# Gate groups moved between the up-projection tiles, one-hot rows built on VectorE, low parts on GpSimd

## What is computed

```python
s = jnp.einsum('thpd,hpnd->thpn', q, sub_keys).astype(jnp.float32)
sv, si = lax.top_k(s, K)
cand = (sv[:, :, 0, :, None] + sv[:, :, 1, None, :]).reshape(T, H, K * K)
...
best, pos = lax.top_k(cand, K)
...
gate = jax.nn.softmax(best, axis=-1).astype(x.dtype)
...
    a = jnp.einsum('chkd,cd->chk', expert_u[ec], xc)
    w = gc * jax.nn.gelu(a, approximate=False)
    return jnp.einsum('chk,chkd->cd', w, expert_v[ec])
```

## Time and profile before

| | |
|---|---|
| median of 3 runs | 2197.05 us (2192.01 to 2198.41) |
| span of the profiled execution | 2194.3 us (its device time is not listed apart; the median lies 2.75 us above the span) |
| PE busy | 2136.5 us, 97% of the span |
| DVE, ACT, POOL busy | 68%, 53%, 8% of the span |
| up-projection of layer 1 | 296 to 664 us of the span |
| gate stage of layer 1 | 664 to 746 us |
| down-projection of layer 1 | 746 to 1088 us |

### The profile page before, as it was taken

How to read it: one execution, slowest core, us unless ns; L and a number is a source line. 1 busy time by engine, 2 the same in 40 slices (tenths; PEclk the granted TensorE clock), 3 DMA queues, 4 the chain that set the end, 5 groups by cost and what they waited for, 6 DMA issues and landing times.

```text
span 2194.3 us, 41496 instructions
## 1 busy us (share of the span) xinstructions
PE 2136.5 (97%) x14244; PEld 1917.2 (87%) x14244; DVE 1500.2 (68%) x2796; ACT 1156.8 (53%) x1835; POOL 181.5 (8%) x202
## 2 busy tenths in 40 slices
PE   8999999999999999999999999999999999999997
PEld 6987899999997788888788888999999977888886
DVE  6666767777778855555676566777777797555556
ACT  4456445544458755445444464444544596444443
POOL 1100000000007400000020000000000182000000
PEclk9999999999999999999999999999999999999999
DMA  5622455555550256666565234555555503665664
GB/s 187 198 86 88 155 165 182 182 183 183 182 180 27 59 191 193 201 203 198 160 197 167 88 106 154 166 183 183 183 183 182 166 0 101 195 201 191 200 204 134
DMA packets 97584, 350.24 MB, mean 160 GB/s; under 512 B 11312, under 2 KB 11344, under 8 KB 97520
## 3 DMA queue, kind: packets, MB, share of 16 engines
q1 hardware_dynamic: 94320, 338.69, 48.3%
q0 software_dynamic: 3200, 10.66, 1.6%
HBM read 348.26 MB, written 1.05 MB: 159 GB/s over the span
## 4 chain that ended last, share of the span: by engine, by line
PE 85%; DMA 4%; DVE 4%; ACT 2%; issue 2%; POOL 1%; POOLq 0%; DVEq 0%; SPq 0%; ACTq 0%
PE wide L1536 33%; PE acc L1521 13%; PE acc L1522 13%; PE acc L1523 13%; PE acc L2003 4%; DMA raw<-in_front 2%; DMA raw<-in_peer_v 2%; PE tr L1714 1%; POOL hot_i L574 1%; ACT hot_i L844 1%; PE acc L1874 1%; ACT hi L601 1%; PE acc L1876 1%; PE acc L1875 1%; PE wide L1972 1%
## 5 line engine op out<-in xcount | busy, mean ns | idle before, releaser
L601 ACT ACTIVATE hi<-raw 128x1024 fp32r<-128x1024 f32 (+1 forms) x644 | 676.3, 1051 | 540.7 <-DMA raw<-in_peer_v 341.9
L919 DVE TENSOR_TENSOR lo<-raw,hi 128x1024 fp32r<-128x1024 f32 x520 | 636.8, 1225 | 448.6 <-ACT hi L601 445.6
L1521 PE MATMUL acc<-xT_hi,lo 128*128 128x256 f32 x2544 | 724.9, 285 | 5.9 <-DVE kr L1132 3.2
L1522 PE MATMUL acc<-xT_lo,hi 128*128 128x256 f32 x2544 | 721.1, 283 | 0.0
L1523 PE MATMUL acc<-xT_hi,hi 128*128 128x256 f32 x2544 | 721.0, 283 | 0.0
L1521 PEld LDWEIGHTS acc<-xT_hi,lo 128*128 128x128 f32 x2544 | 489.4, 192 | 12.6 <-issue 4.6
L1522 PEld LDWEIGHTS acc<-xT_lo,hi 128*128 128x128 f32 x2544 | 489.6, 192 | 0.0
L1523 PEld LDWEIGHTS acc<-xT_hi,hi 128*128 128x128 f32 x2544 | 489.5, 192 | 0.0
L1536 PE MATMUL wide<-hi,w_lo 128*128 128x512 f32 x1016 | 313.9, 390 | 5.4 <-DVE w_lo L1462 5.2
L1536 PE MATMUL wide<-lo,w_hi 128*128 128x512 f32 x1016 | 312.9, 389 | 0.0
L1536 PE MATMUL wide<-hi,w_hi 128*128 128x512 f32 x1016 | 312.8, 389 | 0.0
(11 more groups left out here) (307 smaller groups left out, 1943.2 us busy)
## 6 DMA issues: line engine op xcount, KB each, us to landing
raw<-in_peer_u SPq DMA_DIRECT2D x256, 512.0 KB, 3.5
raw<-in_peer_v SPq DMA_DIRECT2D x254, 512.0 KB, 3.5
raw<-in_front SPq DMA_DIRECT2D x114, 512.0 KB, 3.5
ln_par<-in_ln POOLq DMA_DIRECT2D x10, 512.0 KB, 5.6
raw<-in_front SPq DMA_DIRECT2D x12, 384.0 KB, 3.2
w<-in_cmp_w POOLq DMA_DIRECT2D x16, 256.0 KB, 4.3
raw<-in_front SPq DMA_DIRECT2D x8, 312.0 KB, 3.4
xs<-in_x SPq DMA_DIRECT2D x2, 512.0 KB, 4.6
```

Source lines behind the costliest of these rows:

```text
L601: nc.scalar.activation(hi[:, s, :width], raw[:, s, :width], ACT.Identity).then_inc(hi_done, 1)
L919: nc.vector.tensor_tensor(lo[:, s], raw[:, s], hi[:, s].bitcast(F32), ALU.subtract).then_inc(lo_done, 1)
L1521: mm(dst, lo[:, s, c], xh[:, k], start=k == 0, stop=False)
L1522: mm(dst, hi[:, s, c], xl[:, k], start=False, stop=False)
```

## The change

The 64 gate groups are no longer a stage of their own. They stand one by one behind the up-projection tiles 60 to 123, on TensorE into the PSUM buffer `tr`. For this the routing must be complete by tile 57, so VectorE does its 16 routes one after another from the start of the up-projection. VectorE no longer subtracts low parts there: GpSimd does that for the 125 tiles 3 to 127. VectorE builds both one-hot matrices itself, one token at a time with `tensor_scalar`; the steps on GpSimd and ScalarE and the spreading matmuls are gone. Since gates and Gelu results now arrive in either order, ScalarE fills the parts of `big` of tiles 60 to 127 with ones (34 activations), the Gelu results of these tiles go to one of two buffers `act`, and VectorE multiplies both into `big`. ScalarE waits for 4, 8 and 12 finished routes at tiles 36, 40 and 44, and for all 16 at tile 56.

```diff
@@ gpsimd @@
-                def differences(i, e):
-
-                    toks = picksT[:, 0, bass.ds(i * (4 * HOTS) + 4 * e, 4)].unsqueeze(2).broadcast_to([P, 4, P])
-                    nc.gpsimd.tensor_tensor(rows_i(i, e), iota[:].unsqueeze(1).broadcast_to([P, 4, P]), toks,
-                                            ALU.subtract).then_inc(differences_ready, 1)
...
+                for k in range(POOL_FIRST, NKEYS):
+                    n = T_U + k
+                    s = n % SLOTS
+                    pool.wait_ge(hi_done, l * NT + n + 1)
+                    nc.gpsimd.tensor_tensor(lo[:, s], raw[:, s], hi[:, s].bitcast(F32), ALU.subtract).then_inc(pool_lo, 1)
@@ scalar @@
+                def gelu_tile(k):
+
+                    n = T_U + k
+                    tile_used(l, n // SLOTS, n % SLOTS)
+                    if k < G0:
+                        dst = big[:, k // JB, :, k % JB]
+                    else:
+                        if k >= G0 + 2:
+                            act.wait_ge(tile_times, l * N_TIMES + k - G0 - 1)
+                        dst = acts[k % 2][:].rearrange("p (g t) -> p g t", t=TB)
+                    nc.scalar.activation(dst, acc[:, k % 2, :SEQ].rearrange("p (g t) -> p g t", t=TB),
+                                         ACT.Gelu).then_inc(acc_read[k % 2], 1)
...
+                for k in range(NKEYS):
+                    gelu_tile(k)
+                    if k > 0:
+                        after_gelu(k)
+                    if k in ones_at:
+                        if ones_at[k] >= N_ONES - 8:
+                            unit_done = 4 * ((ones_at[k] - (N_ONES - 8)) // 2 + 1)
+                            act.wait_ge(route_step, (l * 16 + unit_done) * ROUTE_STEPS)
+                        fill_ones(ones_at[k])
+                    if k == 56:
+                        act.wait_ge(best_ready, l + 1)
@@ vector @@
+                for i in range(TT * HEADS):
+                    route(i)
...
+                def rows(m):
+
+                    if m >= 2:
+                        dve.wait_ge(gates_out, l * NG + m - 1)
+                    for r in range(4):
+                        t = 4 * m + r
+                        nc.vector.tensor_scalar(hot_i[:, m % 2, r], iota[:], picksT[:, 0, t:t + 1], None, ALU.is_equal)
+                        ins = nc.vector.tensor_scalar(hot_j[:, m % 2, r], iota[:], picksT[:, 1, t:t + 1], picksT[:, 2, t:t + 1],
+                                                      ALU.is_equal, ALU.mult)
+                    ins.then_inc(hot_ready, 1)
...
+                for m in range(NG):
+                    if m > 0:
+                        dve.wait_ge(gates_read, 2 + l * NG + m)
+                    times_tile(G0 + m)
+                    if m + 2 < NG:
+                        rows(m + 2)
+                    times_gates(m)
@@ tensor @@
+                def gates_of(i, e):
+
+                    pe_.wait_ge(hot_ready, l * NG + (i * 8 + (e + 1)))
+                    pe_.wait_ge(gates_read, l * NG + (i * 8 + (e + 1)))
+                    for r in range(4):
+                        ins = mm(tr[:, e % 2, r * P:(r + 1) * P], hot_i[:, e % 2, r], hot_j[:, e % 2, r], start=True, stop=True)
+                    ins.then_inc(gates_out, 1)
...
+                with pe_.Fori(0, NG // 8) as i:
+                    for e in range(8):
+                        u_tile_of(i, G0, e)
                         gates_of(i, e)
```

More of the change, by code:

```diff
@@ L827, in _ @@
[L827 to L835, removed]
-                def distances(i, e):
-                    act.wait_ge(differences_ready, l * NG + (i * HOTS + (e + 1)))
-                    nc.scalar.activation(rows_i(i, e), rows_i(i, e), ACT.Abs).then_inc(distance_done, 1)
@@ L1332, in _, with route @@
                 dve.sem_inc(apart, 1)
-                def route(i, turn, splits):
+                def route(i):
                     rt = Steps(dve, route_step, (l * 16 + i) * ROUTE_STEPS, ROUTE_STEPS, apart)
@@ L1373, in route @@
-                    assert sum(map(len, stages)) == ROUTE_STEPS
-                    split_after = [round((len(stages) - 1) * (e + 0.5) / len(splits)) for e in range(len(splits))]
-                    for g, stage in enumerate(stages):
-                        for ins in stage:
-                            rt.mark(ins())
-                        for e in splits:
-                            if split_after[e - splits[0]] == g:
-                                after_route(turn, e)
-                        rt.settle()
@@ L1382, in route @@
[L1382 to L1392 removed]
+                    for p in range(2):
+                        rt.mark(nc.vector.max(r_v[:, p, 0:8], scores[p]))
@@ new lines, in route @@
+                    rt.settle()
+                    for p in range(2):
+                        rt.mark(nc.vector.match_replace(r_s2[:, p], r_v[:, p, 0:8], scores[p], LOWEST))
+                    for p in range(2):
+                        rt.mark(nc.vector.max_index(r_i[:, p, 0:8], r_v[:, p, 0:8], scores[p]))
+                    rt.settle()
+                    for p in range(2):
+                        rt.mark(nc.vector.max(r_v[:, p, 8:16], r_s2[:, p]))
+                    rt.settle()
+                    rt.mark(nc.vector.tensor_tensor(
+                        r_c[:].rearrange("p (a b) -> p a b", a=TOPK), r_v[:, 0].unsqueeze(2).broadcast_to(kk),
+                        r_v[:, 1].unsqueeze(1).broadcast_to(kk), ALU.add))
@@ new lines, in route @@
+                    for p in range(2):
+                        rt.mark(nc.vector.max_index(r_i[:, p, 8:16], r_v[:, p, 8:16], r_s2[:, p]))
+                    rt.settle()
+                    rt.mark(nc.vector.max(r_best[:, 0:8], r_c[:]))
+                    rt.mark(nc.vector.tensor_copy(r_if[:], r_i[:]))
+                    rt.settle()
+                    rt.mark(nc.vector.match_replace(r_c2[:], r_best[:, 0:8], r_c[:], LOWEST))
+                    rt.mark(nc.vector.max_index(r_pos[:, 0:8], r_best[:, 0:8], r_c[:]))
@@ new lines, in gates_of @@
+                def gates_of(i, e):
[4 more added lines that the diff above has]
+                    ins.then_inc(gates_out, 1)
+                for k in range(8):
+                    u_tile(k)
+                with pe_.Fori(0, 6) as i:
@@ L2020, in _ @@
-                step(2 * half - 1, None)
+                with pe_.Fori(0, NG // 8) as i:
+                    for e in range(8):
+                        u_tile_of(i, G0, e)
+                        gates_of(i, e)
+                for k in range(G0 + NG, NKEYS):
+                    u_tile(k)
                 pe_.sem_inc(apart, 1)
@@ L2054 @@
 DVE_STEPS = 74
-ROUTE_STEPS = 25
+ROUTE_STEPS = 24
 def lay_out(a):
```

372 lines of the change are left out of this document (118 added, 254 removed).

## The result

| | before | changed |
|---|---|---|
| median | 2196.24 us (4 runs, 2192.01 to 2198.41) | 2444.55 us (4 runs, 2443.18 to 2446.31) |
| span of the profiled execution | 2194.3 us | 2441.5 us |

The ratio is 1.113, with a 95% interval of 1.1114 to 1.1145: slower by 248 us. The forecast was 2386 us with a range of 2235 to 2500.

The account below looks back on a forecast made before the run. TensorE, busy 97% of the span, was taken as the bound. Per layer +48 stall +5 clock and group start +123 gate tiles -81.6 old gate stage = +94; two layers +189 on 2194.3 gave 2383, median 2386 us, range 2235 to 2500.

Parts of the forecast that it names:

- GpSimd's operation: GpSimd's subtraction of 1024 elements per up-projection tile: taken as 2.2 us, with 1.66 and 2.9 as ends.
- a route settles on 5 tiles, 14.4 us: VectorE's routing beside GpSimd in the up-projection: each route takes a whole number of tiles, 4, 5 or 6; 14.4 us taken.
- The undisturbed 9.9: Length in us of one VectorE route without GpSimd beside it; sixteen are 159 us, against tile 56 ending at 161.
- The stall of TensorE: Up-projection: ScalarE stops at tiles 44 and 56 for unfinished routes, TensorE too; 48 us a layer, ends 20 and 66.
- The clock: TensorE's lower clock after a quieter stretch; two stops and the start of the groups together cost 5 us a layer.
- Gate tile, p = 4.8: Up-projection tiles with a gate group: period 4.8 us instead of 2.88 a tile, 123 us a layer over 64 groups.
- TensorE waits for `hot_ready`: Gate tiles: TensorE waits in each for the one-hot rows, 64 x (4.8 - 2.88) = 123 us.
- The stage started at 296.0: Kernel before: start of the up-projection, from 128 tiles of 2.88 us, 368.6 us, before the first gate matmul at 664.65.
- at no cost: ScalarE's 34 fills, the seven tiles without groups at either end and the hand-over to the down-projection: no added time.
- faster, 2158: Rival: exclusion does not slow a chain of short operations, VectorE's pending one goes first; gate tile 3.85, 2158 us; chance 0.12.
- Routing fits, groups don't: Rival: routing stall 0 to 20 us, gate tile 4.3 us, +10 to +30 a layer, 2215 to 2257 us; chance 0.12.
- GpSimd itself is the bound: Rival: GpSimd's operation 2.9 us plus VectorE's exclusions, +142 us a layer, 2480 us; chance 0.10.

Follow-up runs that it names:

- the shortened operations of 256 columns: Changed kernel with GpSimd subtracting only 256 of 1024 columns: 2156.07 us in all tiles, 2321.36 in tiles below 60, 2288.64 in tiles from 60.
- freeing four of them: Changed kernel with the routing's shift, mask, cast of both and best-value subtraction taken off the SBUF-only form: 2414.59 us, ratio 1.0995.
- the four banks: Changed kernel with the gates of the groups going to four PSUM banks in turn instead of two: 2444.07 us, ratio 1.1127.
- the PSUM kernels: Changed kernel, GpSimd's operations at full length, VectorE operands moved to PSUM: groups alone 2288.01 us, groups and routing 2155.68 us.

## Why the prediction was right, and where it was off

The sign and the mechanism held: VectorE's SBUF-only operations and GpSimd's take turns, ScalarE stops for the routes, and TensorE waits in each gate tile. The kernels with the exclusion lifted show it by themselves. The opening has the engines meet only at semaphores; these two also meet at SBUF. The sum was 58 us short, step by step:

- **GpSimd's operation**, taken as 2.2, was 2.40. The straight line's 1.66 was far off, four times the first price too; twice the 512 form was nearer. The Trainium skill's figure (GPSIMD Engine Reference, "Elementwise — side-by-side cycle accounting"), an estimate of 2.25, was nearer still, and low by 0.15. It is the halving that was off, since a part of the operation does not shrink: the shortened operations of 256 columns took 0.80 in the mean, which with 2.40 for 1024 makes an estimate of 0.53 for each 256 columns and 0.27 besides, and so 4.5 for 2048.
- **Routing, "a route settles on 5 tiles, 14.4 us"** was the mis-sized term: 17.2, six tiles. The prediction reckoned with the long steps and left the five short ones as "add to it if they exclude too". They do, and freeing four of them gave 15.4. The undisturbed 9.9 was right: in the stops, with GpSimd idle, routes ended 9.94 apart. The stall of TensorE came out as 60.3 instead of 48, near the 66 that the prediction gave for six tiles, and fell on three stops, with tile 40, which it didn't name, among them. The clock took 5.9, where it had 5 with the start of the groups.
- **Gate tile, p = 4.8** was 5.0: the groups cost 135.3 a layer instead of 123. The formula holds with 2.4 in place of 2.2 and 0.2 us more for rows that stand 0.22 to 0.23 apart, not 0.195. That TensorE waits for `hot_ready` was wrong, it waits for the product with the gates; the four banks showed that this changes nothing.
- **"The stage started at 296.0"** was worked out from a count of matmuls and was 4.4 us late; the row says 291.65. It made the stage before too short, and with it the forecast of the loss too large by 4.4 a layer.
- **Down-projection "at no cost"**: 7.4 a layer, from the place of `w_hi` and `w_lo`.

Layer 1: 94.4 forecast, +13.3 routing and clock, +12.3 gate tiles, -4.4, +7.4 makes 123.0; measured were 115.7 and 7.4, 123.1. Layer 2 lost 123.9.

The rival "faster, 2158" named the size of what exclusion hides: with exclusion lifted, 2155.7. Its condition (a route under 10.1 us) was nearly met at 10.16, and the gate tile was 3.76, below the 3.85 of the prediction. Its mechanism was wrong: VectorE's pending operation did not go first, it waited. The rival "Routing fits, groups don't" falls with the 66.3 lost in the routing. The rival "GpSimd itself is the bound" falls with the PSUM kernels, where it is as long as ever. The lock as the Trainium skill states it (SBUF — State Buffer, "Who interferes with whom") agrees with the stretched rows: the later one is blocked until the other ends. The rows add that it holds down to 16 elements.

## What to carry to other kernels

Before work goes to GpSimd, count what VectorE does beside it that stays within SBUF: each such step may wait for a whole GpSimd operation, even a step of 16 elements. Putting one operand of each of these steps in PSUM, where there is room, made the same plan go from 11% slower to 1.8% faster, and to 2.8% with `w_hi` and `w_lo` back in their places. And when a change rearranges buffers, compare the durations of matmuls that it does not touch: 6 ns each on 3000 of them were 14 to 18 us here.

## What was not expected of the hardware

- Within SBUF and beside GpSimd's operation, a subtraction of 16 elements took up to 1.96 us, a mask of 16 up to 2.41 and a cast of 32 up to 2.38, for 0.22, 0.17 and 0.18 without it. The maximum, find and replace steps and the reduction kept their 0.28 to 0.69 us throughout.
- With `w_hi`, stationary in two of three products, at 194 or 195 KB of the kernel's part of SBUF, all three products of the down-projection were recorded with 394 to 396 ns; with it at 128 or 144 KB with 389 to 390, at a granted clock of 1.00 in both. The weight loads took 188 ns in either case. With `xT_lo`, a moving operand of the up-projection, up instead, the up-projection lost nothing.
